# One Trainium2 core: the last stage of a hybrid mLSTM and attention layer gets its first two chunks loaded while attention ends

## The reference

```python
def reference(x, c, w_ada, b_ada, g_pre, w_in, ..., w_out, g_post):
    mod = jax.nn.silu(c) @ w_ada + b_ada
    shift, scale, gate = jnp.split(mod, 3, axis=-1)
    h = _rmsnorm(x, g_pre) * (1.0 + scale[:, None, :]) + shift[:, None, :]
    proj = h @ w_in
    ...
    h_ml = _mlstm(ml_q, ml_k, ml_v, i_pre, f_pre)
    h_ml = jax.nn.sigmoid(ml_o) * h_ml
    h_ml = _rmsnorm(h_ml, g_ml_head) * jax.nn.silu(ml_z)
    h_sb = _stick_breaking(sb_q, sb_k, sb_v) * jax.nn.silu(sb_z)
    y = jnp.concatenate([h_ml, h_sb], axis=-1) @ w_out
    return x + gate[:, None, :] * _rmsnorm(y, g_post)
```

## Time and profile before

| what | value |
|---|---|
| median of 3 runs | 3584.32 us (3583.04 to 3586.93) |
| the profiled execution's own time | 3586.79 us |
| its span in the profile | 3585.0 us |
| busy over the span: PE, DVE, ACT, POOL | 97%, 70%, 54%, 18% |
| last copy of attention's result ends | 3040.7 us |
| first instruction of the last stage | 3043.0 us |
| first matmul of chunk 0 | 3057.6 us |

### The profile page before, as it was taken

How to read it: one execution, slowest core, us unless ns; L and a number is a source line. 1 busy time by engine, 2 the same in 40 slices (tenths; PEclk the granted TensorE clock), 3 DMA queues, 4 the chain that set the end, 5 groups by cost and what they waited for, 6 DMA issues and landing times. The chain is left out here.

```text
span 3585.0 us, 66410 instructions
## 1 busy us (share of the span) xinstructions
PE 3476.4 (97%) x24179; PEld 2814.5 (79%) x24179; DVE 2496.0 (70%) x3510; ACT 1943.1 (54%) x4045; POOL 649.3 (18%) x676
## 2 busy tenths in 40 slices
PE   7997999999999999989999999999999999799998
PEld 4776888999999978867777777777777776688887
DVE  4674445344688862349889988998999897566665
ACT  4553123222444432237778777877787777455554
POOL 1332332100000024300102010201020103232332
PEclk9999999999999999999999999999999999899999
DMA  8989779777756689850012001200120001666664
GB/s 279 330 314 323 249 264 328 258 231 246 270 185 189 214 294 320 291 191 19 19 48 83 19 19 48 83 19 19 48 78 16 10 31 35 190 195 206 197 209 130
DMA packets 415584, 582.24 MB, mean 162 GB/s; under 512 B 35568, under 2 KB 298096, under 8 KB 414288
## 3 DMA queue, kind: packets, MB, share of 16 engines
q1 hardware_dynamic: 395184, 507.28, 43.5%
q0 software_dynamic: 16960, 58.73, 4.7%
q10 hardware_dynamic: 3168, 12.58, 0.9%
HBM read 393.74 MB, written 184.75 MB: 161 GB/s over the span
## 5 line engine op out<-in xcount | busy, mean ns | idle before, releaser
L1454 DVE TENSOR_TENSOR_SCAN a_prod<-a_keep,a_prod,a_zeros 128x512 f32<-128x512 f32 x896 | 1076.8, 1268 | 94.6 <-ACT a_keep L1370 92.1
L1379 ACT COPY a_turned<-a_rt 128x512 f32<-128x512 f32 x1088 | 546.9, 588 | 238.5 <-PE a_rt L1324 238.1
L1370 ACT ACTIVATE a_keep<-a_z 128x512 f32<-128x512 f32 (+3 forms) x1152 | 555.4, 573 | 40.8 <-PE a_z L1313 40.4
L1324 PEld LDWEIGHTS a_rt<-a_ident,a_prod 128*128 128x128 f32 x4224 | 451.5, 140 | 116.8 <-issue 55.9
L1324 PE MATMUL a_rt<-a_ident,a_prod 128*128 128x128 f32 x4224 | 530.9, 278 | 7.3 <-DVE a_prod L1454 6.7
L1335 PE MATMUL a_acc<-a_turned,a_dw 128*64 128x256 f32 x4352 | 519.7, 380 | 0.7 <-ACT a_osum L1389 0.7
L1335 PEld LDWEIGHTS a_acc<-a_turned,a_dw 128*64 128x64 f32 x4352 | 286.7, 136 | 212.7 <-issue 91.7
L1313 PE MATMUL a_z<-a_khi,a_q 64*128 64x512 f32 (+3 forms) x2304 | 372.4, 402 | 1.3 <-DVE a_xe L1440 0.9
L930 DVE TENSOR_TENSOR p_hlo<-p_wraw,p_hlo 128x1024 fp32r<-128x1024 f32 x85 | 105.2, 1238 | 322.2 <-ACT p_hlo L695 322.2
L695 ACT CAST p_hlo<-p_wraw 128x1024 fp32r<-128x1024 f32 x85 | 89.1, 1049 | 394.6 <-PE p_bank L565 212.9
L1269 POOL TENSOR_SCALAR_AFFINE_SELECT a_keep<-a_keep 128x256 f32<-128x256 f32 x128 | 72.2, 567 | 1244.2 <-ACT a_keep L1370 1241.0
(11 more groups left out here) (303 smaller groups left out, 6292.7 us busy)
## 6 DMA issues: line engine op xcount, KB each, us to landing
p_hlo<-scratch_parts SPq DMA_DIRECT2D x130, 512.0 KB, 5.1
p_wraw<-scratch_sums SPq DMA_DIRECT2D x128, 512.0 KB, 6.6
p_aslot<-scratch_parts SPq DMA_DIRECT2D x62, 512.0 KB, 4.8
p_u<-in_w_in POOLq DMA_DIRECT2D x64, 256.0 KB, 5.5
scratch_wsums<-p_u POOLq DMA_DIRECT2D x32, 512.0 KB, 7.0
p_hraw<-scratch_sbv POOLq DMA_DIRECT2D x32, 512.0 KB, 7.6
m_xt<-in_x SPq DMA_DIRECT2D x32, 512.0 KB, 4.9
out_y<-m_ot SPq DMA_DIRECT2D x32, 512.0 KB, 3.7
```

The source lines that it names most:

```text
L1324: last = pe.transpose(rt[k % RB][:, h * QW + i * P:h * QW + (i + 1) * P], prod[:, u % PB, 2 * i + h, kb * P:(kb + 1) * P], ident[:])
L1370: act.activation(keep[:, at % KB, 0:w], z[at % ZB][:, 0:w], ACT.Sigmoid, scale=-Z_SCALE).then_inc(keep_done, 1)
L1379: act.copy(by_head(turned[:, k % TB]), by_head(rt[k % RB][:])).then_inc(turned_done, 1)
L1454: dve.tensor_tensor_scan(prod[:, u % PB, s, 0:w][:, ::-1], keep[:, at % KB, 0:w][:, ::-1], zeros[:, 0:w], first, ALU.mult, ALU.add).then_i ...
```

## The change

Attention's last step but two, the one at the last pair with `c == 2`, is followed by the loads of chunks 0 and 1 of the last stage, seven for each chunk: all but attention's own result sbt. They go into parts of `khi`, `klo` and `dw` that the remaining rows do not use any more; these tiles, the pair of weight buffers, the identity, the ones and the mask are now held across both stages. The input tiles of the last stage are views into them for all chunks. The two broadcast rows are loaded into the weight buffers between the last two stores of attention. The wait for the last stores is moved from the end of attention to the beginning of the last stage, where SP loads sbt of chunks 0 and 1 behind it and then x of both. sbt has a semaphore of its own. The gate row is made, in chunk 0, behind the scores (PE) and behind pm (DVE). POOL makes the mask at the beginning of attention.

```diff
             for g in range(NP * NCH):
...
                 store(row)
+                if row == NP * NCH * 2 - 2:
+                    sp.wait_ge(wout_step, 8 * KT)
+                    sp.dma_start(wout_raw, b_ada[2 * D:3 * D]...to_broadcast([P, D])).then_inc(held["c_in"], 16)
+                    sp.wait_ge(wgate_step, 8 * KT)
+                    sp.dma_start(wgate, g_post...to_broadcast([P, D])).then_inc(held["c_in"], 16)
                 store(row + 1)
                 if hp + 1 < NP:
                     load_keys(hp + 1, c)
-            for p in range(2):
-                sp.wait_ge(o_st[p], 16 * NP * NCH)
-            sp.wait_ge(m_out, 16)
+                elif c == 2:
+                    sp.wait_ge(m_out, 16)
+                    for chunk in range(2):
+                        load_mix(sp, d, mix_in, chunk, chunk, held["ch_in"])
...
+def load_mix(sp, d, mix_in, c, p, ch_in):
+    rows = slice(c * P, (c + 1) * P) if isinstance(c, int) else bass.ds(c * P, P)
+    by_head = lambda t: t[rows, :].rearrange("t (h e) -> t h e", h=MH)
+    sp.dma_start(mix_in["mb"][:, p], d["m"][:, rows].unsqueeze(0).to_broadcast([P, MH, P])).then_inc(ch_in[p], 16)
+    sp.dma_start(mix_in["kT"][:, p], d["mlk"][c]).then_inc(ch_in[p], 16)
+    sp.dma_start(mix_in["qT"][:, p], d["mlq"][c]).then_inc(ch_in[p], 16)
+    sp.dma_start(mix_in["v"][:, p, :, 0:MD], by_head(d["v"])).then_inc(ch_in[p], 16)
+    sp.dma_start(mix_in["so"][:, p], by_head(d["so"])).then_inc(ch_in[p], 16)
+    sp.dma_start(mix_in["szg"][:, p], by_head(d["szg"])).then_inc(ch_in[p], 16)
+    sp.dma_start(mix_in["gz"][:, p], d["sbz"][:, rows].rearrange("(k p) t -> p k t", p=P)).then_inc(ch_in[p], 16)
...
-            load(0, 0)
-            load_x(0, 0)
-            load_x(1, 1)
-            for tile, row in ((ot[:, 0], b_ada[2 * D:3 * D]), (ot[:, 1], g_post)):
-                sp.dma_start(tile, row.rearrange("(a n) -> a n", a=1).to_broadcast([P, D])).then_inc(e["c_in"], 16)
+            for p in range(2):
+                sp.wait_ge(o_st[p], 16 * SH // 2 * NCH)
+            for p in range(2):
+                load_sb(p, p)
+            for p in range(2):
+                load_x(p, p)
...
-                if not last:
+                if not last and not (isinstance(c, int) and c == 0):
...
-                    load(c + 1, 1 - p)
+                    load_mix(sp, d, mix_in, c + 1, 1 - p, ch_in)
+                    load_sb(c + 1, 1 - p)
...
         @block.tensor
         def _(pe):
-            pe.wait_ge(e["const"], 6)
-            for nb in range(2):
-                last = pe.matmul(y_ps[nb][:], ones[:], gate_sum[:, nb * CH:(nb + 1) * CH], start=True, stop=True)
-            last.then_inc(e["g_done"], 1)
...
                 turn_and_score(c, half, p)
                 first = isinstance(c, int) and c == 0
+                if first:
+                    for nb in range(2):
+                        last = pe.matmul(y_ps[nb][:], ones[:], gate_sum[:, nb * CH:(nb + 1) * CH], start=True, stop=True)
+                    last.then_inc(e["g_done"], 1)
...
                 dve.tensor_tensor(pm[:], s_ps[:], dwt[:], ALU.mult).then_inc(e["pm_done"], 1)
-                if not first:
+                if first:
+                    gate_rows()
+                    gate_sb(half, p)
+                else:
                     low_h(c - 1)
...
+        view = lambda tile, k: held[tile][:, 2 * k * CH:2 * (k + 1) * CH].bitcast(F32).rearrange("p (a h t) -> p a h t", a=2, h=MH)
+        mix_in = dict(qT=view("khi", 1), kT=view("khi", 2), mb=view("khi", 3), so=view("klo", 1), szg=view("klo", 2), gz=view("klo", 3))
```

More of the change, by code:

```diff
@@ L1100, in _, with stage_attend @@
             assert next_w == len(PIECES)
-def stage_attend(nc, d, cols, wout_hi, wout_lo, w_out, csil, w_ada, gate_sum):
+def stage_attend(nc, d, cols, wout_hi, wout_lo, w_out, csil, w_ada, gate_sum, b_ada, g_post, held, mix_in, o_st):
     NP = SH // 2
@@ L1491, in stage_mix @@
         e = {n: sem(n) for n in names}
-        ch_in, x_in, out_st = ([sem(f"{n}{p}") for p in range(2)] for n in ("ch_in", "x_in", "out_st"))
+        x_in, out_st, sb_in = ([sem(f"{n}{p}") for p in range(2)] for n in ("x_in", "out_st", "sb_in"))
+        ch_in = held["ch_in"]
         block = ctx.enter_context(nc.Block())
@@ L1562, in _ @@
         def _(pool):
-            identity(pool, ident[:], e["const"], 0)
-            pool.memset(maskb[:], 0.0).then_inc(e["const"], 1)
-            pool.wait_ge(e["const"], 3)
-            pool.affine_select(out=maskb[:], in_=maskb[:], compare_op=ALU.is_ge, fill=BIG, base=0,
-                               pattern=[[1, P]], channel_multiplier=-1).then_inc(e["const"], 1)
-            pool.memset(v[:, :, :, MD:VW], 1.0).then_inc(e["const"], 1)
-            pool.memset(state[:], 0.0).then_inc(e["state_done"], MH)
-            pool.memset(ones[:], 1.0).then_inc(e["const"], 1)
+            pool.memset(v[:, :, :, MD:VW], 1.0).then_inc(e["state_done"], MH - 1)
+            pool.memset(state[:], 0.0).then_inc(e["state_done"], 1)
             def body(c, half, p):
-                after(pool, ch_in[p], 128 * half + 128)
+                after(pool, ch_in[p], 112 * half + 112)
                 after(pool, e["wq_done"], MH * (c + 1))
@@ L1701, in body @@
                     act.activation(kn[:, h], t_ps[:, h], ACT.Copy, scale=dyn(cols["wk"], h)).then_inc(e["kn_done"], 1)
-                after(act, ch_in[p], 128 * half + 128)
+                after(act, ch_in[p], 112 * half + 112)
                 after(act, e["qs_done"], c)
@@ L1740, in _, with gate_rows, gate_sb @@
                 dve.sem_inc(out_st[p], 16)
-            dve.wait_ge(e["c_in"], 32)
-            dve.wait_ge(e["g_done"], 1)
-            for nb in range(2):
-                cc = slice(nb * CH, (nb + 1) * CH)
-                dve.tensor_tensor(ggb[:, cc], y_ps[nb][:], ot[:, 0, cc], ALU.add).then_inc(e["g_step"], 1)
-            dve.wait_ge(e["g_step"], 2)
-            dve.tensor_tensor(ggb[:], ggb[:], ot[:, 1], ALU.mult).then_inc(e["g_step"], 1)
-            dve.wait_ge(e["g_step"], 3)
-            dve.wait_ge(e["const"], 4)
+            def gate_rows():
+                dve.wait_ge(held["c_in"], 32)
+                dve.wait_ge(e["g_done"], 1)
+                for nb in range(2):
+                    cc = slice(nb * CH, (nb + 1) * CH)
+                    dve.tensor_tensor(ggb[:, cc], y_ps[nb][:], ot[:, 0, cc], ALU.add).then_inc(e["g_step"], 1)
+                dve.wait_ge(e["g_step"], 2)
+                dve.tensor_tensor(ggb[:], ggb[:], ot[:, 1], ALU.mult).then_inc(e["g_step"], 1)
+                dve.wait_ge(e["g_step"], 3)
+            def gate_sb(half, p):
+                after(dve, sb_in[p], 16 * half + 16)
+                dve.tensor_tensor(sbt[:, p], sbt[:, p], gz[:, p], ALU.mult).then_inc(e["gate_done"], 1)
             def newton(step, base, r0, var, t1, t2, r, n):
@@ L1781, in body @@
                 first = isinstance(c, int) and c == 0
-                after(dve, ch_in[p], 128 * half + 128)
-                dve.tensor_tensor(sbt[:, p], sbt[:, p], gz[:, p], ALU.mult).then_inc(e["gate_done"], 1)
+                after(dve, ch_in[p], 112 * half + 112)
+                if not first:
+                    gate_sb(half, p)
                 after(dve, e["dwt_done"], c)
```

78 lines of the change are left out of this document (39 added, 39 removed).

## The result

The changed kernel took 3566.27 us (median of 5 runs, 3562.82 to 3567.54), the kernel before on the same chip 3585.26 us (5 runs, 3583.04 to 3587.94): a ratio of 0.9942, with a 95% interval of 0.9931 to 0.9952. It is faster, as forecast, by 19.0 us; 21.4 were expected.

The account below looks back on a forecast made before the run. Bound: the last stage's start, where VectorE waits 28.2 us for g_post and TensorE 8.9 us for chunk 0's loads. Span 3585.0 - 21.4 = 3563.6 us; against the median 3562.9 us, range 3560.3 to 3571.

Parts of the forecast that it names:

- The middle is 3036.6, and I take that the data are there.: Fourteen early loads of chunks 0 and 1: landed between 3028.4 and 3044.7, so before the last stage's start at 3041.6.
- The first rival, stuck stores: End of attention: row 62's copy waits for store 60 behind the loads; costs 0 to 6 us, middle 3; chance 0.15.
- Last stage at 3041.6: Border of the stages: start at 3041.6 instead of 3042.99, without SP's 1.4 us wait for the last store.
- Two broadcast issues between the stores, nothing: SP's queue at attention's end: two broadcast issues priced at nothing, though up to 1.3 us could stick out.
- The mark 8.2 to 10.5 us after the start, middle 9.3: VectorE's dneg of chunk 0, the mark: between 3049.8 and 3052.1, middle 3050.9, with the stage starting at 3041.6.
- The clock: TensorE at the last stage's start: low level by the skill's rule alone, a 20.3 us gain; middle of both levels taken.
- sbt "just in time" at 3049: Chunk 0's sbt: issued after the last store lands at 3045.5, then a lone load of about 3.5 us.
- Rival two: Before dneg of chunk 0: VectorE waits for sbt or broadcasts, gain only 14.3 to 19, about 3567 us; chance 0.08.
- TensorE low for longer: Chunk 0's first projections: clock stays at 0.50, leaving 14 us of gain, 3570 us; chance 0.05.
- Slower: Last stage's loop: VectorE waits for sbt, now last of eight loads, in each of 30 chunks; 3592 us; chance 0.02.
- Nothing gained: Start of the last stage: the kernel still waits as long for another thing; chance 0.02.
- From the mark on unchanged: From dneg of chunk 0: 9.2 us to pm of chunk 1 unchanged, earlier gains then carried unchanged to the end.

Follow-up runs that it names:

- gate row first: Changed kernel with gate products back ahead of the transposes, gate row and gate of sbt ahead of gap: 3569.56 us, one run.
- wait before barrier: Changed kernel with the wait for the last stores back at the end of attention, ahead of the barrier: 3570.64 us, one run.
- spread loads: Changed kernel with the fourteen early loads issued in smaller groups, each once its place is dead: 3563.65 us, run again 3563.12 us.
- four osum buffers: Changed kernel with four osum buffers instead of two, early loads left in place: 3561.51 us, one run.

## Why the prediction was right, and where it was wrong

The direction, the mechanism and the range held. The median is 3.4 us above the forecast: 0.9 of it is that the kernel before itself ran at 3585.26 instead of 3584.32, and 2.4 are gain that is missing (19.0 instead of 21.4). One step failed, and it costs about that or somewhat less. In the tail of the profiled execution only 0.55 us are missing, since other terms came out better than forecast: the start was 1.3 us late, and 0.7 us were gained behind the mark, where nothing was expected. Point by point, with the prediction's times moved by the 1.55 us that this execution was late from the beginning:

- *"The middle is 3036.6, and I take that the data are there."* **This is the step that failed.** The last load was issued at 3033.70, and loads of this kind landed in some 7 us (medians of 6.0 to 7.4 by tile), so at about 3041, 3 us behind the middle (3038.1 with the shift). I had priced the 14 issues at a pace of data, not at SP's time: SP was held for 13.3 us, and the stores stood behind it. The first rival, stuck stores, is what happened, with a price of 1.4 to 1.7 us at the stage's start (24.42 and 24.70 against 23.03 and 23.02) and of 1.8 to 2.6 in the tail (544.74 less 542.97; 545.65 less 543.27 or 543.08), where I had 0 to 6, middle 3. What lies between the two is mostly the clock behind the start. In all four executions where a copy waited for a store (after twice, gate row first, wait before barrier) the stage began at the low level; of the six others that had their loads by then two did (the first of the spread loads, four osum buffers). Whether the store's wait brings the low level with it is not shown. I gave it 0.15; it needed no more than that the loads, and store 60 behind them, be later than row 62's copy, and two of my three landing times (3036.6, 3044.7) lay within 2 us of that or behind it. Its chance should have been a half or so.
- *The Trainium skill's rule on the ring order* ("DMA: Bandwidth & Descriptors", "Queues, rings and completion order"), which I set beside that rival: the trace agrees, a store behind the loads took 6.9 us instead of 1.8.
- *Last stage at 3041.6* (3043.15 with the shift): 3044.47. The moved wait did what was expected, the 1.39 us of the stuck store took its gain away; without it the start is at +23.03, and 3041.6 stood for +23.1.
- *Two broadcast issues between the stores, nothing*: right. The last store left at 3043.66, as the copy of row 63 ended (3043.01 + 0.62).
- *The mark 8.2 to 10.5 us after the start, middle 9.3*: 9.26, but not in the way I had it. I had two cases, all of TensorE's work at the low level with the gate row hidden under n, or all of it at the high level with the gate row as the bound. In fact the products were slow, until 3050.44, n was fast, and the gate row's 3.2 us stood behind the products. The other execution of the same kernel, with faster products, had the mark at 7.93. The middle was met by chance; the lower end, 8.2, by its mechanism (7.93 with VectorE without a pause).
- *The clock.* The sentence from the Trainium skill ("TensorE: Matmul & The Clock Gate", "What's actually happening"), that the throttled state is the default and activity releases it, was read as the low level at the new start. In this execution that is what the rows show; in the second execution of the spread loads the clock stayed at 1.00 over a pause of 1.54 us of TensorE. So the rows bear that reading out in some executions only.
- *sbt "just in time" at 3049* (3050.6 with the shift): issued at 3048.46, landed in 2.6 to 3.3 us, so by some 3051.8, 1.3 us ahead of its use at 3053.12. The 3.5 us that I took for a lone load stand in no row shown (the trace of before has 3.3 and 3.5, medians, for attention's last key loads); here it took 2.6 to 3.3. With the spread loads VectorE did not wait for it in front of the mark either. Rival two did not come true: VectorE waited for TensorE's products, not for the broadcasts (3.9 and 5.0 us to landing).
- *TensorE low for longer*: no, 1.00 from 3050 on. *Slower*: VectorE waited once, 1.3 us in chunk 2, for sbt in the loop, and TensorE never for it. *Nothing gained*: no.
- *The readings.* 393 GB/s is not the fullest stretch of before: the next one has 408 (columns as in the earlier trace rows), which would put the lower end of the loads' landing at 3028.1 instead of 3028.4; nothing hangs on it.

```profile
3057.00:3059.00 2.00, 1.41 (x7) 1.41 (x8) 0.00 (x0) 0.17 (x1) 0.00 (x0) 0.50 1.03 408
```

- *From the mark on unchanged*: right to pm of chunk 1, 9.20 us in both, and not quite behind it: to the end it is 511.97 us, before 512.64. VectorE's pm of chunks 2 and 31, before and then after (timelines):

```profile
3096.66 0.69 DVE L1793 TENSOR_TENSOR m_pm<-mp_s,m_dwt 128x512 f32<-128x512 f32 x1 [0.76 <-ACT m_dwt L1709]
3551.04 0.69 DVE L1793 TENSOR_TENSOR m_pm<-mp_s,m_dwt 128x512 f32<-128x512 f32 x1 [0.70 <-ACT m_dwt L1709]
...
3078.48 0.69 DVE L1799 TENSOR_TENSOR m_pm<-mp_s,m_dwt 128x512 f32<-128x512 f32 x1 [0.86 <-ACT m_dwt L1709]
3531.83 0.69 DVE L1799 TENSOR_TENSOR m_pm<-mp_s,m_dwt 128x512 f32<-128x512 f32 x1 [0.70 <-ACT m_dwt L1709]
```

Chunk 2, where VectorE waits for sbt, comes 0.45 us later behind the mark (24.75 against 24.30), and the 29 chunks behind it take 453.35 us instead of 454.38. Three other executions with the changed loop have 453.4 too, so these 1.0 us belong to the changed kernel, as far as one execution of before can tell; why its loop is 0.035 us shorter for a chunk stays open.

## What to carry to other kernels

A prefetch that nobody waits for still has a price: what stands behind it on its issuing queue. Count the issues at the time that a long row of them takes (here 14 in 13.3 us, not 14 times 0.43), and ask which small store behind them frees a buffer; issuing each load when its place is dead, or a deeper ring of buffers, brought the stage's start 1.4 to 1.7 us forward. When a wait at a stage's start is removed, what follows is bound by short work whose length hangs on the clock, so forecast it by its order on each engine, not by two extreme levels. And a wait in a table of totals says nothing of its place: the wait for sbt that an expectation here put in chunk 0 was in chunk 2.

## What was unexpected of the hardware

SP's issue instructions themselves grew to some 2 us (2.28, 1.83, 2.02) in a row of 14 loads of 256 KB, instead of 0.43; in the spread loads, four in a row after step 2, none took more than 0.47. The granted clock after one and the same pause of TensorE at the border of the stages, 1.5 us, was near 0.50 in one execution of a kernel and 1.00 in another: the spread loads had 0.54 and 0.61 from their stage's start in the first, 1.00 in the second. It cost 0.3 us there. In the changed kernel both executions began at 0.50, and the one in which the clock rose later had its mark 1.33 us later. A pause of 3.55 us in front of n brought 0.50 only while n was running.
